# Attention with keys on partitions, a separate product for the maxima, and the next head prepared between steps

## The reference, cut

```python
def mla_mixer(u, w_in, q_norm, kv_norm, w_q_up, w_kv_up, q_head_norm, k_head_norm, w_out):
    c_q, c_kv, k_rope = jnp.split(u @ w_in, [Q_LORA_RANK, Q_LORA_RANK + KV_LORA_RANK], axis=-1)
    q = (rmsnorm(c_q, q_norm) @ w_q_up).reshape(b, L, MLA_HEADS, QK_HEAD_DIM)
    kv = (rmsnorm(c_kv, kv_norm) @ w_kv_up).reshape(b, L, MLA_HEADS, QK_NOPE_DIM + V_HEAD_DIM)
    k_nope, v = jnp.split(kv, [QK_NOPE_DIM], axis=-1)
    k = jnp.concatenate([k_nope, broadcast(k_rope)], axis=-1)
    q, k = apply_rope(rmsnorm(q, q_head_norm), pos), apply_rope(rmsnorm(k, k_head_norm), pos)
    p = jax.nn.softmax(q @ k.T / math.sqrt(QK_HEAD_DIM), axis=-1)   # per head and sequence
    return (p @ v).reshape(b, L, MLA_HEADS * V_HEAD_DIM) @ w_out
```

## Time and profile before

| | us |
|---|---|
| median of 3 runs | 3584.16 (3580.08 to 3591.8) |
| the profiled execution, its time | 3577.84 |
| its span, first to last instruction | 3575.7 |
| PE busy | 3360.7 (94%) |
| DVE busy | 1790.0 (50%) |
| POOL busy | 1339.2 (37%) |
| ACT busy | 732.9 (20%) |
| mean granted TensorE clock | 0.957 of full speed |

### The profile page before, as it was taken

The page is one execution under the profiler, slowest core; times in us unless marked ns, Lnnn a source line. Parts: engine busy times, 40 slices in busy tenths (PEclk is TensorE's granted clock), DMA queues, the critical chain, the costliest instruction groups (busy, mean ns, idle before and its releaser), DMA issues.

```text
span 3575.7 us, 51239 instructions
## 1 busy us (share of the span) xinstructions
PE 3360.7 (94%) x20670; PEld 2980.3 (83%) x20670; DVE 1790.0 (50%) x2301; ACT 732.9 (20%) x1213; POOL 1339.2 (37%) x602
## 2 busy tenths in 40 slices
PE   7999999999999999999899999789997799999996
PEld 7888888888999999999899987556666688888885
DVE  5555555556433333333578881378786533333334
ACT  3333333334100000000211121233333200000001
POOL 4111111111334444444334443366775244444441
PEclk9899999999999999999999999989999899999997
DMA  2000000000111111111223322423322111111111
GB/s 105 25 13 13 13 13 13 13 13 34 69 36 47 47 41 47 47 41 47 77 79 93 111 94 82 139 71 105 113 89 89 51 48 47 47 47 47 47 47 59
DMA packets 111503, 202.10 MB, mean 57 GB/s; under 512 B 7285, under 2 KB 55669, under 8 KB 111349
## 3 DMA queue, kind: packets, MB, share of 16 engines
q1 hardware_dynamic: 71728, 149.97, 12.6%
q10 hardware_dynamic: 39621, 49.83, 4.1%
HBM read 164.38 MB, written 35.39 MB: 56 GB/s over the span
## 4 chain that ended last, share of the span: by engine, by line
PE 83%; DVE 7%; POOL 4%; issue 3%; ACT 2%; ACTq 1%; DMA 0%; DVEq 0%; POOLq 0%
PE PS L626 79%; PE PS L769 3%; POOL Wlo L549 1%; DVE SS L1480 1%; POOL SQ L594 1%; POOL RMS L559 1%; ACT ZB L1352 1%; PE PS L894 0%; POOL SQ L589 0%; DVE H L1692 0%; PE PS L1024 0%; DVE H L2026 0%; DVE H L2025 0%; DVE SMAX L1634 0%; POOL STF L573 0%
## 5 line engine op out<-in xcount | busy, mean ns | idle before, releaser
L522 POOL TENSOR_TENSOR Whi<-Wraw,const 128x1024 fp32r<-128x1024 f32 x203 | 491.8, 2423 | 1995.1 <-PE PS L626 1987.8
L626 PE MATMUL PS<-Uhi,Whi 128*128 128x352 f32 (+1 forms) x2504 | 618.3, 347 | 55.9 <-DVE Ulo L1492 49.8
L626 PE MATMUL PS<-Ulo,Whi 128*128 128x352 f32 (+1 forms) x2504 | 611.3, 345 | 0.0
L626 PE MATMUL PS<-Uhi,Wlo 128*128 128x352 f32 (+1 forms) x2504 | 609.8, 344 | 0.0
L525 POOL TENSOR_TENSOR Wlo<-Wraw,Whi 128x1024 fp32r<-128x1024 f32 x203 | 550.8, 2713 | 15.9
L626 PEld LDWEIGHTS PS<-Uhi,Whi 128*128 128x128 f32 x2504 | 438.8, 190 | 91.6 <-issue 36.2
L626 PEld LDWEIGHTS PS<-Uhi,Wlo 128*128 128x128 f32 x2504 | 444.1, 189 | 31.3
L626 PEld LDWEIGHTS PS<-Ulo,Whi 128*128 128x128 f32 x2504 | 441.3, 189 | 30.6
L1692 DVE TENSOR_TENSOR H<-H,PS 128x1056 f32<-128x1056 f32 (+1 forms) x176 | 217.8, 1238 | 270.1 <-PE PS L626 270.1
L1711 DVE TENSOR_TENSOR HID<-PS,RMS 128x1056 f32<-128x1056 f32 (+1 forms) x44 | 54.6, 1241 | 451.8 <-PE PS L626 451.8
L1266 ACT ACTIVATE HIDhi<-HID 128x1056 fp32r<-128x1056 f32 (+1 forms) x44 | 47.3, 1074 | 1014.7 <-DVE HID L1716 1014.7
(11 more groups left out here) (242 smaller groups left out, 5025.8 us busy)
## 6 DMA issues: line engine op xcount, KB each, us to landing
Wraw<-in_w SPq DMA_DIRECT2D x219, 512.0 KB, 3.5
xt<-XTT ACTq DMA_DIRECT2D x20, 640.0 KB, 5.7
H<-in_x ACTq DMA_DIRECT2D x16, 528.0 KB, 8.9
Wraw<-in_w SPq DMA_DIRECT2D x32, 256.0 KB, 3.1
zt<-ZB ACTq DMA_DIRECT2D x32, 256.0 KB, 2.0
X<-xt SPq DMA_DIRECT2D x8, 1024.0 KB
Z<-zt SPq DMA_DIRECT2D x32, 256.0 KB, 2.7
saved<-H ACTq DMA_DIRECT2D x8, 528.0 KB, 5.0
```

The lines of the kernel that those rows point to most:

```text
L522: pool.tensor_tensor(Whi[s][:], Wraw[s][:], ones.unsqueeze(1).broadcast_to([P, BLK, P]), ALU.mult)\
L626: ins = pe.matmul(out, lhsT, rhs, start=start, stop=stop, skip_group_check=True)
```

## The change

Attention alone is rewritten, without loops. The 528 keys of a sequence are taken in `KB` = 5 blocks of `CW` = 106 partitions (the last overlaps by two, which are masked). A step t is one head, one sequence, one half of 264 queries and one block of keys, 20 per head, 320 in all: `scores` makes three split products and a fourth that subtracts the queries' shift (MINUS x SHIFT), ACT takes the exponential straight into PT in the layout that the next product wants, and `outputs` multiplies it in plain fp32 with a stationary operand of 64 columns V and 64 columns of ones, so that 64 partitions of the result hold the attended values and 64 the sum. Transposes and copies of the probabilities are gone. Every five steps `take_attended` (DVE) takes a reciprocal of 64x264 sums and multiplies with it.

The shift of each query is the maximum over high-part scores, from a separate product (`block_scores`, queries on partitions, 106 x 528, into the bank group A_PREP), a maximum on DVE, a transpose (`turn_maxima`) and `shift_rows`, which writes the rows of SHIFT.

The next head is prepared between the steps of this one, in an order written out for PE, ACT and DVE; in PE's loop `nxt` is the head whose factors and maxima are made, `after` the one whose Q (and K for each second one, V for each fourth) is projected. The bank group A_PREP (banks 4 to 6) is used by K, Q, V, both factor spreads and all maxima in turn; `prep_orders` numbers these uses, and `wait_prep` makes each wait until all earlier ones are taken (`prep_taken`). Norm sums use bank 7 in the same way (`stats_taken`). KHI and QHI are made by ACT, KLO and QLO by DVE, Q is turned by POOL. V is projected for four heads at a time. Around attention, sums by token are taken by parts of 106, and the loader's order follows. Lines that are left out are marked; the left-out functions mirror those shown.

```diff
+CW = 106
+KB = 5
+KW = NSEQ * KB
+QHALF = L // 2
+PER_HEAD = NSEQ * 2 * KB
+A_SCORE, A_OUT, A_PREP, A_STAT = 0, 2, 4, 7
+PROBS = 4
+SHIFTS = 3
...
+def key_start(w):
+    return w // KB * L + min(w % KB * CW, L - CW)
...
+            wait_prep("v", g, part)
+            for w in range(6 * part, (6, KW)[part]):
+                i = w - 6 * part
+                for kt in range(KKV):
+                    for p, (Xs, W) in enumerate(((Chi, Whi), (Chi, Wlo), (Clo, Whi))):
+                        ins = mm(PS[0:CW, A_PREP + i // 2, i % 2 * 2 * P:(i % 2 + 1) * 2 * P],
+                                 Xs[:, KQ + kt, key_start(w):key_start(w) + CW], W[s][:, kt:2 * KKV:KKV, :],
+                                 start=(kt == 0 and p == 0), stop=(kt == KKV - 1 and p == 2))
+            ins.then_inc(prep_full, 1)
...
+        def key_norms(p):
+            pe.wait_ge(prep_taken, PREP["k", p] + 1)
+            wait_stats("k", p)
+            sums_by_part(A_STAT, 0, SS, mask(M_KE, 2)).then_inc(stats_full, 1)
...
+        def spread(factor):
+            for w, lo, hi in pieces:
+                ins = mm(PS[:, A_PREP + lo // NT, lo % NT:lo % NT + hi - lo],
+                         factor[:, w:w + 1].broadcast_to([CW, P]), ident[0:CW, lo - key_start(w):hi - key_start(w)])
+            ins.then_inc(prep_full, 1)
...
+        def spread_queries(x):
+            pe.wait_ge(qs_ready, x + 1)
+            wait_prep("qs", x)
+            spread(TOK[:, K_QS, :])
+        def block_scores(x, s, b):
+            if s == 0 and b == 0:
+                pe.wait_ge(k_hi, x + 1)
+                pe.wait_ge(q_hi, x + 1)
+            wait_prep("max", x, s, b)
+            at = key_start(KB * s + b)
             for h in range(2):
+                ins = mm(PS[0:CW, A_PREP + h, 0:QHALF], QHI[x % 2][:, at:at + CW],
+                         KHI[x % 2][:, s * L + h * QHALF:s * L + (h + 1) * QHALF])
+            ins.then_inc(prep_full, 1)
+        def turn_maxima(x, s):
+            pe.wait_ge(prep_taken, PREP["max", x, s, KB - 1] + 1)
+            wait_stats("max", x, s)
+            pe.transpose(PS[0:KB, A_STAT, 0:CW], SMAX[:, s, :], ident[0:CW, 0:CW]).then_inc(stats_full, 1)
...
+        def scores(t):
+            m, b = divmod(t, KB)
+            x, s, h = m // 4, m // 2 % 2, m % 2
+            if t >= 2:
+                pe.wait_ge(p_ready, t - 1)
...
+            if b == 0 and h == 0:
+                pe.wait_ge(stats_taken, STATS["max", x, s] + 1)
+            at = key_start(KB * s + b)
+            of = slice(s * L + h * QHALF, s * L + (h + 1) * QHALF)
+            out = PS[0:CW, A_SCORE + t % 2, 0:QHALF]
+            mm(out, KHI[x % 2][:, at:at + CW], QHI[x % 2][:, of], stop=False)
+            mm(out, KHI[x % 2][:, at:at + CW], QLO[x % 2][:, of], start=False, stop=False)
+            mm(out, KLO[x % 2][:, at:at + CW], QHI[x % 2][:, of], start=False, stop=False)
+            mm(out, MINUS[:], SHIFT[:, m // 2 % SHIFTS, h * QHALF:(h + 1) * QHALF], start=False).then_inc(sc_full, 1)
+        def outputs(t):
+            m, b = divmod(t, KB)
+            x, s = m // 4, m // 2 % 2
+            pe.wait_ge(p_ready, t + 1)
+            if b == 0 and m >= 2:
+                pe.wait_ge(att_taken, m - 1)
+            pe.matmul(PS[:, A_OUT + m % 2, 0:QHALF], V[x // 4 % 2][:, KB * s + b, x // 2 % 2, x % 2 * VD:x % 2 * VD + P],
+                      PT[:, t % PROBS, :], start=(b == 0), stop=(b == KB - 1), skip_group_check=True).then_inc(pv_done, 1)
...
+        project_k(0)
+        project_q(0)
+        project_v(0, 0)
+        project_v(0, 1)
+        wait_prep("rope")
+        spread(TOK[:, K_RB, :])
+        pe.wait_ge(minus_ready, 2)
+        for j in range(-1, HEADS):
+            nxt, after = j + 1, j + 2
+            for i in range(PER_HEAD):
+                t = j * PER_HEAD + i
+                if j >= 0:
+                    scores(t)
+                if nxt < HEADS:
+                    if i == 0 and nxt and nxt % 4 == 0:
+                        project_v(nxt // 4, 1)
+                    if i == 0 and nxt % 2 == 0:
+                        key_norms(nxt // 2)
+                    if i == 1:
+                        query_norms(nxt)
+                    if i == 2:
+                        spread_keys(nxt)
+                    if i == 4:
+                        spread_queries(nxt)
+                    if 8 <= i < 8 + KB:
+                        block_scores(nxt, 0, i - 8)
+                    if i == 8 + KB:
+                        turn_maxima(nxt, 0)
+                    if 8 + KB <= i < 8 + 2 * KB:
+                        block_scores(nxt, 1, i - 8 - KB)
+                    if i == 8 + 2 * KB:
+                        turn_maxima(nxt, 1)
+                if after < HEADS:
+                    if i == 18 and after % 2 == 0:
+                        project_k(after // 2)
+                    if i == 19:
+                        project_q(after)
+                        if after % 4 == 0:
+                            project_v(after // 4, 0)
+                if t >= 2:
+                    outputs(t - 2)
+        for t in range(HEADS * PER_HEAD - 2, HEADS * PER_HEAD):
+            outputs(t)
...
+        def take_k(p):
+            act.wait_ge(prep_full, PREP["k", p] + 1)
...
+            act.activation(banks(KR[0][0:NOPE, :]), prepared[0:NOPE], ACT.Copy, scale=col("k_nope")[0:NOPE])\
+                .then_inc(act_steps, c.adds(act_steps))
+            act.activation(banks(KR[1][NOPE:P, :]), prepared[NOPE:P], ACT.Copy, scale=col("k_nope")[NOPE:P])\
+                .then_inc(act_steps, c.adds(act_steps))
+            act.activation(banks(SS[:]), prepared, ACT.Square).then_inc(prep_taken, 1)
+        def take_q(x):
+            act.wait_ge(prep_full, PREP["q", x] + 1)
...
+            act.activation(banks(QR[:]), prepared, ACT.Copy).then_inc(prep_taken, 1)
+            act.wait_ge(prep_taken, PREP["q", x] + 1)
...
+            act.activation(SQ[:], QR[:], ACT.Square).then_inc(q_squared, 1)
+        def high_k(x):
+            act.wait_ge(prep_taken, PREP["ks", x] + 1)
...
+            act.activation(KHI[x % 2][:], SS[:], ACT.Copy).then_inc(k_hi, 1)
+        def high_q(x):
+            act.wait_ge(prep_taken, PREP["qs", x] + 1)
+            act.activation(QHI[x % 2][:], QR[:], ACT.Copy).then_inc(q_hi, 1)
+        def exponentials_of(t):
+            act.wait_ge(sc_full, t + 1)
+            if t >= PROBS:
+                act.wait_ge(pv_done, t - PROBS + 1)
+            act.activation(PT[:, t % PROBS, :], PS[0:CW, A_SCORE + t % 2, 0:QHALF], ACT.Exp).then_inc(p_ready, 1)
...
+        for j in range(-1, HEADS):
+            nxt, after = j + 1, j + 2
+            for i in range(PER_HEAD):
+                if j >= 0:
+                    exponentials_of(j * PER_HEAD + i)
+                if nxt < HEADS:
+                    if i == 5:
+                        high_k(nxt)
+                    if i == 6:
+                        high_q(nxt)
+                if after < HEADS:
+                    if i == 18 and after % 2 == 0:
+                        take_k(after // 2)
+                    if i == 19:
+                        take_q(after)
...
+            pool.wait_ge(q_squared, x + 1)
...
+            pool.tensor_tensor(seqs(QR[:]), seqs(QR[:]), trig_q[:, x % 2, :].unsqueeze(1).broadcast_to([P, NSEQ, L]),
+                               ALU.mult).then_inc(q_turned, 1)
...
+        def key_factors(p):
+            vec.wait_ge(stats_full, STATS["k", p] + 1)
+            vec.tensor_tensor(tok(K_V, 2), part_sum(A_STAT, 0, 2), pairwise(K_B2), ALU.mult).then_inc(stats_taken, 1)
+            vec.wait_ge(stats_taken, STATS["k", p] + 1)
+            step(vec.tensor_tensor(tok(K_V, 2), tok(K_V, 2), pairwise(K_RR), ALU.add))
+            rsqrt(tok(K_KF, 2), tok(K_V, 2), tok(K_TMP, 2))
...
+            vec.tensor_tensor(KS[:], tok(K_KF, 2), pairwise(K_B), ALU.mult).then_inc(ks_ready, 1)
+        def query_factors(x):
+            vec.wait_ge(stats_full, STATS["q", x] + 1)
+            vec.tensor_tensor(tok(K_V), part_sum(A_STAT, 0), tok(K_A2), ALU.mult).then_inc(stats_taken, 1)
+            vec.wait_ge(stats_taken, STATS["q", x] + 1)
+            step(vec.tensor_scalar(tok(K_V), tok(K_V), EPS, None, ALU.add))
...
+            rsqrt(tok(K_QS), tok(K_V), tok(K_TMP))
+            step(vec.scalar_tensor_tensor(tok(K_QS), tok(K_QS), 1.0 / math.sqrt(QK), tok(K_A), ALU.mult, ALU.mult))
+            vec.sem_inc(qs_ready, 1)
...
+        def scale_queries(x):
+            vec.wait_ge(prep_full, PREP["qs", x] + 1)
+            vec.wait_ge(q_turned, x + 1)
+            vec.tensor_tensor(banks(QR[:]), banks(QR[:]), prepared, ALU.mult).then_inc(prep_taken, 1)
...
+        def low_q(x):
+            vec.wait_ge(q_hi, x + 1)
+            vec.tensor_tensor(QLO[x % 2][:], QR[:], QHI[x % 2][:].bitcast(F32), ALU.subtract).then_inc(q_lo, 1)
+        def block_maximum(x, s, b):
+            vec.wait_ge(prep_full, PREP["max", x, s, b] + 1)
...
```

(51 more changed lines are left out.)

550 lines of the change are left out of this document (270 added, 280 removed).

## The result

The changed kernel takes 3763.1 us (median, 3761.1 to 3765.9), the kernel before 3582.2: ratio 1.050, 95% interval 1.048 to 1.052. It is slower, as forecast, but by 181 us where 107 were expected; the time lies inside the range, near its upper end, and 28 us above the forecast's own narrower range (3640 to 3735).

What follows compares the result with a forecast made beforehand. PE sets the pace before; afterwards it waits for the preparation. The stretch's 820.6 against 759 us gives +62, clock 45, together +107 on 3577.8: 3685, taken as 3690 at the median. Range 3595 to 3785, own range 3640 to 3735.

Steps and rivals of the forecast that it cites:

- rival 2: Heads: clock low for most of each, steps and spreads double, 3 us more per head; 3735 us, chance 0.19.
- Rival 3: DVE's take_attended: division cheap, 0.96 us in place of 2.33, 82 us less, no clock lost; 3563 us, chance 0.12.
- A step: PE in attention: four split products and one fp32 product, 0.94 us, 320 times, 301 us.
- A spread: PE, factors spread over all columns: 24 records, 2.6 us each, 33 groups, 86 us.
- The start: Ahead of head 0, preparation uncovered: 68 us plus 12 for PE at half clock, 80 us (65 to 90).
- A head whose next one is even: Steady state, no key projection: 44.7 us, 9 to 10 of them PE waits, before 3 us for the clock.
- The waits there: PE waiting for DVE or ACT at five places of a head, 0.7 to 3.3 us each.
- Edits at no cost: POOL's turn of Q and splits, in a head's first 12 us: free, as POOL's queue has 675 us idle.
- a head whose next one is odd: Steady state with project_k and a wait for take_k, no key norms: 48.5 us, before 3 us for the clock.
- The clock term: Heads: slow products after waits and narrow products cost 3 us in each of 15, 45 us (0 to 90).
- Rival 1: Heads: the clock holds, as DVE's waits are short enough; 3645 us, chance 0.22.
- Rival 4: Preparation between steps: runs beside them but isn't hidden; already in the forecast at 9 to 12 us per head.

Runs made afterwards that it cites:

- the first experiment: Changed kernel, with POOL's turn of Q and the splits queued behind it waiting until the query factors are done: 3703.2 us, ratio 1.033.
- the fourth experiment: Changed kernel, with idle PE products before some query spreads, the second block of scores and each transpose of maxima: 3723.1 us, ratio 1.039.
- the spaced kernel: Against the 3601.4 us kernel with deferred divisions and idle products: query norms, both spreads and high parts one step later; 3583.0 us, ratio 0.9992.

## Why the prediction was right, and where it was short

**The range.** The forecast was 3690, its own range ended at 3735, and the measured 3763 lies beyond. That the wide range holds it, up to 3785, is luck: its upper end was set for rival 2's clock, and what filled it was mostly something that the forecast had at nothing.

**The direction, and its ground.** Right: PE's work shrank (590 us of it at full clock by the forecast), and its waits for DVE more than took the place. Its terms one by one:

- The reciprocal of 264 elements: 1.80 forecast, 1.805 measured, 64 times. Rival 3, the cheap division, fell with that. What the division costs in all is shown by its removal, 95 us; the rival had 82 for making it cheap.
- A step: 0.94 forecast. In the last head, with nothing in between, the output products start at 1043.39 and 1044.32: 0.93. A spread: 2.6 forecast; where the clock is 1.00, 2.66 to the start of what follows (491.20 to 493.86), 2.82 with the modelled end.
- The start: 80 forecast; the window of it is 79, at a clock of 0.64.
- A head whose next one is even: 44.7 + 3 = 47.7 forecast, 49.8 to 50.7 measured in the four that have no V.
- The waits there: 1.5 forecast before `spread_queries`, none measured; 3.3 before the second block, 2.9 is the longest; 1.9 at `turn_maxima`, at most 1.6; 0.7 behind `shift_rows`, 0.28; 2.45 for `take_k`, 2.54.
- Outside the stretch nothing changed, as forecast.

**The step that failed** is the first sentence of "Edits at no cost". POOL's turn of Q and its splits were costed at nothing, because POOL waits 675 us and its work lies in the first 12 us of a head. The only thing asked was whether POOL would be late. What its work does to the engine beside it wasn't asked. In a head whose next one is odd the splits of the weights and the turn of Q run from 527.67 to 537.43 us, over most of the chain of query factors. That head takes 59.9 us from its first score to the end of `project_q` (525.47 to 585.37), where 48.5 + 3 = 51.5 were forecast: 8.4 over, and 8.97 - 2.95 = 6.0 of the factor operations and 5.43 - 2.82 = 2.6 of the spread at the clock of 0.50 behind the wait make that up. Not all eight such heads are alike. In the first the chain grows to 6.98 us too, but PE waits only 0.37 and the head takes 51.7, next to nothing over. Three have two splits in place of four and a chain of 7.0 us, and take 59.0 to 59.2. Three, with the one shown, take 59.7 to 60.9. The last one, which projects nothing, has a chain of 11.12 and takes 51.3 where 38.8 + 3 = 41.8 were forecast. Together they are 58 us over. The span is 3759.3 where 3575.7 + 107 = 3682.7 were forecast, 77 over; the remaining 19 lie almost all in the seven heads whose next one is even, 2 to 3 in each, the waits of V with them. There POOL has no splits, and its turn of Q overlaps the key factors' first operations only: in four of the seven, one of them takes 1.78 us (L1830).

The first experiment shows it from the other side, and prices it: without the overlap the pair of heads is 100.8 us where 99.2 were forecast, and the whole is 3703, 60 us less and 13 from the forecast of 3690. So of the 73 us between forecast and result 60 are this step.

The rows before the prediction couldn't have given the price: the factor operations at 425 us have a POOL that is idle beside them. But the question could have been asked: the forecast itself has POOL's work in the first 12 us of a head and DVE's factor chains, to 8.4 us, in the same stretch. Which operations are held the traces show only afterwards, and no single feature marks them. In the chain above the product of 2.21 us has two inputs from SBUF and the integer operation of 2.28 us has one, and both end within 0.03 us of POOL's. The first of the chain (529.70, 0.17 us), with an input from PSUM, and the second (529.91, 0.20 us), with one from SBUF, pass beside POOL's turn of Q, and in the first experiment the operations with an input from PSUM keep their 1.80 and 1.25 us beside POOL. What decides between them no run shows. The eight chains took 66.0 us together where 8 x 2.95 = 23.6 were forecast, 42 us more.

**The clock term** (3 us per head, 45 in all) was somewhat small. With POOL out of the way, in the first experiment, the four heads whose next one is even and that have no V still take 49.0 to 49.8 us where 47.7 were forecast, though the 1.5 us wait of the forecast isn't there. And it isn't independent of the waits. The waits that POOL made brought more of it (from 192 to 1000 us the granted clock is 0.85 with them and 0.88 in the first experiment, without them), and what the clock costs in the changed kernel is 40 us or more by the fourth experiment. Rival 2 (3735) came nearest to the time, but not for its reason: the 3 us more per head that it gave to the clock are in fact 7.5 to 9.5 in seven of the eight whose next one is odd, and in the one shown 6.0 of them are DVE's longer chain. Rival 1 (the clock holds) fell: 0.85 in the heads.

**Rival 4** (the preparation isn't hidden) was judged right to be in the forecast. That much of it could be hidden, from 3763 to 3547 with every operation of the change still in it, was not seen. It took the order, copies of values and sums on ACT, a copy of K on DVE and idle products at the start. "I see no row for it" was said of full hiding; no full hiding was needed.

## What to carry to other kernels

Before work is called free because its engine is idle, lay it in time beside the engines that it could hold up, and ask which small operations on the critical chain lie in the same microseconds. A chain of many short DVE operations is exposed: in the one shown four of fourteen were held to the end of a POOL operation seven to fourteen times their length, and the chain tripled. And where an engine's queue holds both what another engine is waiting for and what nobody needs yet (here the divisions), the second kind belongs behind the first, even if it takes a copy on a third engine to free the buffer: here that was worth about 90 us (ratio 1.033 to 1.009, 3703.2 to 3611.6, with the splits' later place in it).

## What the runs showed of the hardware

- **A small DVE operation beside POOL.** On SBUF operands it took 2.28, 2.21, 1.19 and 1.12 us in place of 0.17, ending with POOL's operation. A longer one is held too: in the spaced kernel one of the sixteen low parts of Q (1056 elements, two SBUF inputs) met a split of POOL that ran to 826.60 and took 3.42 us from 824.30; the other fifteen met none and took 1.26. The low part of K just before it took 3.16 in place of 1.26, and POOL's split, which started under that one, 3.26 in place of 2.37, so each engine held the other. A reciprocal with one SBUF input wasn't held: in the spaced kernel it started at 422.96 inside POOL's turn of Q and took 1.79 us. The timelines, of the reciprocal and then of the low parts, POOL first:

```profile
421.13 2.45 POOL L646 TENSOR_TENSOR QR<-QR,RMS 128x1056 f32<-128x1056 f32 x1 [28.93 <-DVEq L1888]
...
421.79 1.25 DVE L1897 TENSOR_TENSOR SS<-KR,PS 128x1056 f32<-128x1056 f32 x1 [0.87 <-PE PS L734]
...
422.96 1.79 DVE L1941 RECIPROCAL SUM<-SUM 64x264 f32<-64x264 f32 x1
```

```profile
820.89 2.37 POOL L607 TENSOR_TENSOR Whi<-Wraw,const 128x1024 fp32r<-128x1024 f32 x1
823.34 3.26 POOL L610 TENSOR_TENSOR Wlo<-Wraw,Whi 128x1024 fp32r<-128x1024 f32 x1
```

```profile
821.21 3.16 DVE L1908 TENSOR_TENSOR KLO<-SS,KHI 128x1056 fp32r<-128x1056 f32 x1 [1.10 <-ACT KHI L1460]
824.30 3.42 DVE L1913 TENSOR_TENSOR QLO<-QR,QHI 128x1056 fp32r<-128x1056 f32 x1
```

- **The reciprocal** goes at 6.3 ns per element from PSUM (1805 ns for 264, of which 149 are those of a single element) and the same from SBUF (1792 ns), where the copy of the same elements is 430 ns.
- **The order of narrow products changes the granted clock.** The query norms, and all that follows them, one step later, with no work removed, took the clock from 0.90 to 0.97 and 18 us off the time. PE was no busier for it, rather less (730.6 of 800 us where it was 762.9). Why the clock follows that order and not the busy share is left open.
